# First stick-breaking layer: the last eighth of a round's dense tiles moves from ahead of the next logits to behind them

## What is computed

```python
proj = rms_norm(x, norm_g) @ w_in
q, k, v, gate = jnp.split(proj, 4, axis=-1)
...
z = jnp.einsum('bthd,bshd->bhts', q[:, t0:kl], k[:, :kl]).astype(jnp.float32) * scale
mask = s_idx < t_idx
log_fail = jnp.where(mask, jax.nn.log_sigmoid(-z), 0.0)
later = lax.cumsum(log_fail, axis=3, reverse=True) - log_fail
a = jnp.where(mask, jnp.exp(jax.nn.log_sigmoid(z) + later), 0.0)
outs.append(jnp.einsum('bhts,bshd->bthd', a.astype(v.dtype), v[:, :kl]))
...
return x + (o * jax.nn.silu(gate)) @ w_out
```

## Time and profile before

| | |
|---|---|
| median of 3 runs | 1831.23 us (1830.14 to 1832.12) |
| the profiled execution's own time | 1828.41 us |
| its span | 1826.6 us |
| TensorE busy | 1770.9 us, 97% of the span, 10400 matmuls |
| VectorE, ScalarE, GpSimd busy | 1150.4, 877.8, 473.0 us |
| mean granted TensorE clock | 0.997 |

### The profile page before, as it was taken

The page is one execution under the profiler, slowest core; times in us unless marked ns, Lnnn a source line. Parts: engine busy times, 40 slices in busy tenths (PEclk is TensorE's granted clock), DMA queues, the critical chain, the costliest instruction groups (busy, mean ns, idle before and its releaser), DMA issues.

```text
span 1826.6 us, 26395 instructions
## 1 busy us (share of the span) xinstructions
PE 1770.9 (97%) x10400; PEld 1461.6 (80%) x10404; DVE 1150.4 (63%) x1861; ACT 877.8 (48%) x1433; POOL 473.0 (26%) x467
## 2 busy tenths in 40 slices
PE   7999999998899999999999999999999999999997
PEld 6877777776788757677879898988888787989896
DVE  5355556575546688854578575765677656858574
ACT  5236665466535365564345252633445534435253
POOL 0035551014411145560130000005678214000000
PEclk9999999999999999999999999999999999999999
DMA  5321111231012321111232322222222123232322
GB/s 177 101 73 54 48 47 58 81 99 53 24 54 102 126 62 34 33 36 58 81 125 83 116 93 104 92 94 82 87 92 75 48 84 125 81 116 93 107 90 81
DMA packets 44522, 149.22 MB, mean 82 GB/s; under 512 B 6000, under 2 KB 6384, under 8 KB 44400
## 3 DMA queue, kind: packets, MB, share of 16 engines
q1 hardware_dynamic: 44400, 147.53, 24.4%
HBM read 139.64 MB, written 2.10 MB: 78 GB/s over the span
## 4 chain that ended last, share of the span: by engine, by line
PE 85%; DVE 6%; ACT 4%; POOL 2%; issue 2%; DMA 0%; POOLq 0%; SPq 0%; DVEq 0%; ACTq 0%
PE BANK L299 18%; PE BANK L301 18%; PE BANK L300 18%; PE BANK L2509 4%; PE BANK L2508 4%; PE BANK L2506 4%; PE BANK L686 2%; PE BANK L1843 1%; PE BANK L1824 1%; PE BANK L1051 1%; PE BANK L1800 1%; PE BANK L2839 1%; PE BANK L671 1%; PE BANK L2814 1%; DVE LH L796 1%
## 5 line engine op out<-in xcount | busy, mean ns | idle before, releaser
L267 ACT ACTIVATE WH<-WRAW 128x1024 fp32r<-128x1024 f32 (+1 forms) x214 | 223.0, 1044 | 327.5 <-PE BANK L301 299.5
L276 DVE TENSOR_TENSOR WL<-WRAW,WH 128x1024 fp32r<-128x1024 f32 (+1 forms) x201 | 255.9, 1274 | 136.3 <-ACT WH L267 136.1
L299 PE MATMUL BANK<-HH,WH 128*128 128x512 f32 x664 | 273.3, 412 | 12.9 <-DVE WL L276 9.7
L301 PE MATMUL BANK<-HL,WH 128*128 128x512 f32 x664 | 260.3, 392 | 0.0
L300 PE MATMUL BANK<-HH,WL 128*128 128x512 f32 x664 | 259.9, 391 | 0.0
L299 PE MATMUL BANK<-HIDH,WH 128*128 128x512 f32 (+1 forms) x520 | 201.2, 387 | 1.6 <-issue 1.5
L300 PE MATMUL BANK<-HIDH,WL 128*128 128x512 f32 (+1 forms) x520 | 200.7, 386 | 0.0
L301 PE MATMUL BANK<-HIDL,WH 128*128 128x512 f32 (+1 forms) x520 | 200.7, 386 | 0.0
L2509 PE MATMUL BANK<-HP,G 128*128 128x256 f32 x672 | 190.2, 283 | 0.0
L2508 PE MATMUL BANK<-HP,G 128*128 128x256 f32 x672 | 190.2, 283 | 0.0
L2506 PE MATMUL BANK<-HP,G 128*128 128x256 f32 x672 | 190.1, 283 | 0.0
(11 more groups left out here) (473 smaller groups left out, 3755.7 us busy)
## 6 DMA issues: line engine op xcount, KB each, us to landing
WRAW<-in_w SPq DMA_DIRECT2D x77, 512.0 KB, 3.5
WRAW<-in_wd SPq DMA_DIRECT2D x64, 512.0 KB, 3.5
RAW<-in_wf SPq DMA_DIRECT2D x32, 512.0 KB, 3.6
WRAW<-in_wu SPq DMA_DIRECT2D x16, 512.0 KB, 3.4
TMP<-in_wf SPq DMA_DIRECT2D x16, 512.0 KB, 3.5
WRAW<-in_w0o SPq DMA_DIRECT2D x8, 512.0 KB, 3.5
WRAW<-in_w1o SPq DMA_DIRECT2D x8, 512.0 KB, 3.6
WRAW<-in_wc SPq DMA_DIRECT2D x8, 512.0 KB, 3.4
```

What stands on the lines that cost most here:

```text
L267: e.activation(WH[b % NS][:, 0:n], WRAW[b % NR][:, 0:n], ACT.Copy).then_inc(*inc("s_high", ("high", b)))
L276: e.tensor_tensor(WL[b % NS][:, 0:n], WRAW[b % NR][:, 0:n], WH[b % NS][:, 0:n].bitcast(F32), ALU.subtract).then_inc(*inc("s_low_pool" if p ...
L299: e.matmul(dst, ah, bh, start=first and i == 0, stop=False)
L301: made = e.matmul(dst, ah, bl, start=False, stop=last and i == len(sets) - 1)
```

## The change

In `l0_tensor`, the rounds m = 0 to 5 end with three eighths instead of four, and one eighth stands behind each of `logits(1)` to `logits(6)`, ahead of the values of the pair before.

```diff
@@ -709,13 +709,15 @@
             for m in range(6):
                 logits(m)
                 if m:
+                    eighths(1)
                     values(m - 1)
                 eighths(8 if m else 12)
                 sums(2 * m)
                 eighths(4)
                 sums(2 * m + 1)
-                eighths(4)
+                eighths(3)
             logits(6)
+            eighths(1)
             values(5)
             eighths(8)
             sums(12)
```

## The result

The changed kernel takes 1839.53 us (median of 6 runs, 1838.71 to 1843.63), the kernel before 1830.68 us over six runs on the same chip. The ratio is 1.0048, with a 95% interval of 1.0032 to 1.0065: 8.85 us slower, where 9.7 had been forecast from the single term of 1.61 us a round.

The account below looks back on a forecast made before the run. Bound by TensorE, 97% busy, with a chain through ScalarE, VectorE and GpSimd ahead of the sums. Six rounds at 1.61 us add 9.7 us to the 1831.23 median: 1840.9 us, range 1837.5 to 1845, chance 0.84.

Parts of the forecast that it names:

- the single term of 1.61 us a round: First-layer loop: magnitudes 2.30 us later against the logits, logits 0.69 us earlier; six rounds cost 9.7 us.
- The chain named in the earlier trace: In each round, waits run from the logits through ScalarE, VectorE and GpSimd to the sums, where TensorE waits 0.48 us.
- The lead of the logits: Moving three matmuls behind the logits starts each set of logits 0.69 us earlier; nothing else they need is late.
- rival B: Logits don't come forward, since exponentials or a low part end late: 2.30 us a round, 13.8 us, 1845.0; chance 0.04.
- The delay of the magnitudes: ScalarE's copy, released later, holds the magnitudes until L + 4.69 instead of L + 2.39; L is the logits' start.
- The wait at the sums: At each round's first sums, TensorE arrives as before but waits 2.09 us instead of 0.48.
- the changeover: Extra operand-shape change on TensorE around the moved eighth: 0.11 us a round, falling into TensorE's wait at no cost.
- The cover: VectorE, GpSimd, bank 7 and the weight loads see the delay too, but it stays hidden; only the sums are late.
- The order on ScalarE: ScalarE takes instructions strictly in order, so the magnitudes never start ahead of the waiting copy.
- A: Rival: no hold on ScalarE, so TensorE loses its 0.48 us wait: 2.9 us gained, time 1828.3; chance 0.06.
- C: Rival: TensorE's clock falls in the loop's longer waits, six falls adding 10.2 us: 1851.1; chance 0.04.
- One sign: Everything behind the first-layer loop was to last as long as before.

Follow-up runs that it names:

- e6: The changed kernel with only VectorE's low half moved behind the high part of k, ScalarE's copy left ahead of the magnitudes: 1839.49 us, against 1831.22 before.
- e8: e3 with ScalarE's copy and VectorE's low half moved later as in e1: 1837.03 us, against 1831.19 before.
- e1: The changed kernel with ScalarE's copy moved behind the second head's logarithm and VectorE's low half behind the high part of k: 1828.11 us, against 1830.60 before.
- e3: The changed kernel with the moved eighth one step later, behind the values instead of ahead of them: 1864.66 us, against 1830.60 before.
- e7: e1 with two eighths in the first round moved ahead of the first sums (14, 3, 2 for 12, 4, 3): 1827.33 us, against 1831.22 before.
- e4: The changed kernel with all tiles one eighth further ahead, five eighths before the first logits and seven behind the loop's last values: 1835.53 us, against 1830.60 before.

## Why the prediction was right

**What bounds.** The chain named in the earlier trace rows bounds the rounds after the change too, with the copy as one more link. Right.

**The lead of the logits.** Forecast 0.69 us. The logits of pair 1 start at 138.03; before, they start at 139.58, less the 0.86 us by which the whole profile was early, 138.72: 0.69. Neither the exponentials nor the low part of k held them (rival B did not come).

**The delay of the magnitudes.** Forecast L + 4.69, measured 166.34 - 161.78 = L + 4.56. The size that was off is mainly the start of the moved eighth: taken from the place of the values at L + 2.68, measured at L + 2.56 (164.34), which is the lower bound of the text (L + 2.57). The values' first matmul before had started 0.12 us later than a dense matmul does in that place. The second matmul came 0.31 us on, not 0.34. With 0.50 in place of 0.49 and 0.96 in place of 0.95 for the two handovers, the delay is 4.56 - 2.39 - 0.69 = 1.48 in place of 1.61 us; the rounds have 1.47, and 6 x 1.47 = 8.8 us. The first logits' rows, after and before:

```profile
138.03 2.19 PE L671 MATMUL BANK<-L0P 64*128 64x512 f32 x24
139.58 2.19 PE L671 MATMUL BANK<-L0P 64*128 64x512 f32 x24
```

**The wait at the sums.** Forecast 0.48 + 1.61 = 2.09 us, with TensorE there at the same time as before. Measured: 2.07 us from the last dense matmul (172.90) to the sums (174.97), less 0.23, so 1.84. Of the 0.25 us that are missing, 0.14 are the smaller term, and 0.11 are TensorE's own: it arrives that much later (0.48 + 1.47 - 1.84 = 0.11). That is the changeover which the text had let fall into the wait, and there it costs nothing.

**The cover.** VectorE, GpSimd, the bank and the weight loads were hidden, as e6, the 2.09 us on VectorE and the dense matmuls behind the values show, which wait for nothing. It was thinner than it sounds: e8 exhausts it by a further delay of the tile's end.

**The order on ScalarE.** The rows of after show that the magnitudes don't pass the waiting copy: the last of the masks' matmuls is over by 163.91 + 0.62 = 164.53, yet ScalarE is idle until the copy starts at 165.38, and the magnitudes start at 166.34. The Trainium skill ("TensorE: Matmul & The Clock Gate", the table's row on queue depth) has ScalarE take its instructions strictly in order. The trace agrees.

**The rivals.** A gave 2.9 us less than before for a copy that doesn't hold; e1, which makes that case, has 2.5 less by the medians and 2.7 by the loop. C did not come: the clock stayed at 1.00 with a wait of 2.07 us between starts in all six rounds. e3 shows that it was real for longer waits, at 1.6 us a fall where the rival had reckoned with 1.7.

**What was luck.** The medians differ by 8.85 us and the loops by 8.79. That closeness is luck: the interval of the ratio stands for 5.9 to 11.9 us, and the two profiles alone differ by 10.3. The round length, 1.47 against 1.61, is the firm comparison. One sign failed in the profile: what is behind the loop was 2.4 us longer than before, through the clock in the second layer.

## What to carry over

An instruction that waits stands in front of all that follow it on its engine, so before moving the work that releases it, look up every engine that waits for that release and what is queued behind the wait. Here one tile's end released a copy on ScalarE that could run 10.9 us later at no cost (e1), and that stood ahead of the first step of the critical chain. The same move pays once the copy is put where its engine is idle (e1, e7), and the same trap stands at the other tile's end (e4).

## What the runs showed of the chip

In the loop the clock stayed up behind the shorter waits and fell behind the longer ones. With 2.07 us from the last dense matmul's start to the sums, the granted clock stayed at 1.00 in six of six rounds. With 3.46 us (a wait of 3.07 in the row) it went to the lower level, 1.2 GHz, in six of six (one of them for longer: that round took 29.03 us at a mean of 0.88), and the sums behind it took 1.6 us more. So in e3 some 10 of the 34 us are clock: the longer wait is paid for twice.

The length of a wait does not settle it, though. In the second layer the same wait (3.14 and 3.15 us) had no fall behind it in the profile of before and one in that of after. And in the profile of after the clock went down behind a wait of 1.52 us, shorter than those in the loop (the matmuls of 128x384 take 0.53 us here); in that of before, the same wait of 1.52 us has 1.00 behind it and the same matmuls take 0.34:

```profile
457.06 0.56 PE L977 MATMUL BANK<-mhi,mqh 128*128 128x384 f32 x1 [1.52 <-ACT SCR L1006]
457.42 0.53 PE L977 MATMUL BANK<-mhi,mql 128*128 128x384 f32 x1
458.00:459.00 1.00, 1.00 (x4) 0.50 0.00 0
...
449.39 0.34 PE L975 MATMUL BANK<-mhi,mql 128*128 128x384 f32 x1
```

That fall cost the program nothing by the next wait (473.57 less 465.68 is 7.89 us, the loop's end 7.93). What decides between a fall and none is not shown here.
